# Latent attention: scores with keys on the partitions in three rounded passes, the row maximum as a 97th feature, sums and scalings on GpSimd

## The reference, cut to what matters

```python
def queries(cq, rotate):
    q = (_rms(cq) * q_norm) @ w_uq
    q = _rms(q.reshape(*q.shape[:2], MLA_HEADS, MLA_QK)) * q_gain
    return _rope_tail(q, cos, sin) if rotate else q

def _block_attention(q, k, v):            # scale = 96 ** -0.5
    s = jnp.einsum('bqhd,bkhd->bhqk', qi, k).astype(jnp.float32) * scale
    p = jax.nn.softmax(s, axis=-1).astype(v.dtype)
    return jnp.einsum('bhqk,bkhd->bqhd', p, v)
```

## Time and profile before

| what | us |
|---|---|
| median of 3 runs | 3493.1 (3488.01 to 3498.14) |
| the profiled execution | 3493.74 |
| its span, first to last instruction | 3492.4 |
| PE busy | 3274.6 (94%) |
| DVE / ACT / POOL busy | 1735.5 / 1314.0 / 1055.9 |
| queries' projection, PE at work without a gap, ends at | 2815.4 |
| first scores | 2823.85 |
| `mla_out_tensor` begins | 3068.37 |

### The profile page before, as it was taken

How to read it: one execution, slowest core, us unless ns; L and a number is a source line. 1 busy time by engine, 2 the same in 40 slices (tenths; PEclk the granted TensorE clock), 3 DMA queues, 4 the chain that set the end, 5 groups by cost and what they waited for, 6 DMA issues and landing times.

```text
span 3492.4 us, 44447 instructions
## 1 busy us (share of the span) xinstructions
PE 3274.6 (94%) x16968; PEld 2608.6 (75%) x16968; DVE 1735.5 (50%) x3222; ACT 1314.0 (38%) x2282; POOL 1055.9 (30%) x513
## 2 busy tenths in 40 slices
PE   8999999999999898999898899999999988889999
PEld 6677777777867777778786577888988556668877
DVE  5458445424138644532798655222565645543234
ACT  4433433333343334334424433222443455533332
POOL 3123131144313222124327332322543000034443
PEclk9999999999999899999999999999999999999999
DMA  5532121133462022123121001221332110022222
GB/s 184 194 127 80 52 89 46 61 101 117 156 227 86 33 71 83 55 83 124 64 67 61 1 31 61 67 67 61 121 109 85 38 36 1 8 72 91 97 97 79
DMA packets 87479, 286.40 MB, mean 82 GB/s; under 512 B 9697, under 2 KB 20321, under 8 KB 86497
## 3 DMA queue, kind: packets, MB, share of 16 engines
q1 hardware_dynamic: 85968, 272.67, 23.1%
q10 hardware_dynamic: 1296, 10.88, 0.8%
HBM read 279.31 MB, written 4.19 MB: 81 GB/s over the span
## 4 chain that ended last, share of the span: by engine, by line
PE 54%; DVE 7%; ACT 3%; issue 2%; POOL 0%; DMA 0%; DVEq 0%; ACTq 0%; POOLq 0%
PE psum L318 14%; PE psum L320 14%; PE psum L319 14%; PE psum L317 9%; PE psum L3796 1%; DVE mla_cols L3885 1%; PE psum L3784 1%; PE psum L1192 1%; DVE h_low L582 0%; PE psum L3762 0%; DVE padded L2834 0%; DVE ml_weights L3237 0%; DVE squares L511 0%; ACT weights_high L395 0%; ACT mla_probs L3841 0%
## 5 line engine op out<-in xcount | busy, mean ns | idle before, releaser
L413 POOL TENSOR_TENSOR weights_low<-weights_loaded,weights_high 128x1024 fp32r<-128x1024 f32 (+3 forms) x456 | 958.4, 2102 | 2350.3 <-ACT weights_high L395 2093.5
L318 PE MATMUL psum<-h_high,weights_high 128*128 128x512 f32 (+1 forms) x2384 | 901.0, 378 | 46.6 <-DVE h_low L582 21.2
L319 PE MATMUL psum<-h_low,weights_high 128*128 128x512 f32 (+1 forms) x2384 | 883.0, 370 | 0.0
L320 PE MATMUL psum<-h_high,weights_low 128*128 128x512 f32 (+1 forms) x2384 | 882.4, 370 | 0.0
L395 ACT CAST weights_high<-weights_loaded 128x1024 fp32r<-128x1024 f32 (+3 forms) x456 | 421.1, 923 | 463.0 <-PE psum L320 392.2
L318 PEld LDWEIGHTS psum<-h_high,weights_high 128*128 128x128 f32 x2384 | 456.2, 191 | 135.4 <-issue 32.6
L319 PEld LDWEIGHTS psum<-h_low,weights_high 128*128 128x128 f32 x2384 | 456.1, 191 | 77.8 <-issue 4.1
L320 PEld LDWEIGHTS psum<-h_high,weights_low 128*128 128x128 f32 x2384 | 454.8, 191 | 76.9
L318 PE MATMUL psum<-act_high,weights_high 128*128 128x512 f32 (+1 forms) x528 | 187.6, 355 | 8.2 <-DVE act_low L4183 6.2
L319 PE MATMUL psum<-act_low,weights_high 128*128 128x512 f32 (+1 forms) x528 | 187.5, 355 | 0.0
L320 PE MATMUL psum<-act_high,weights_low 128*128 128x512 f32 (+1 forms) x528 | 187.4, 355 | 0.0
(11 more groups left out here) (512 smaller groups left out, 5240.8 us busy)
## 6 DMA issues: line engine op xcount, KB each, us to landing
weights_loaded<-stream_dram SPq DMA_DIRECT2D x468, 512.0 KB, 3.3
weights_loaded<-stream_dram SPq DMA_DIRECT2D x80, 128.0 KB, 2.3
weights_loaded<-stream_dram SPq DMA_DIRECT2D x24, 384.0 KB, 3.0
weights_loaded<-stream_dram SPq DMA_DIRECT2D x8, 272.0 KB, 4.6
x<-x_dram SPq DMA_DIRECT2D x4, 512.0 KB, 7.4
arena_mem<-mem_dram ACTq DMA_DIRECT2D x2, 1024.0 KB, 5.9
x<-x_dram ACTq DMA_DIRECT2D x1, 2048.0 KB, 8.4
x_kept_dram<-x ACTq DMA_DIRECT2D x1, 2048.0 KB, 9.8
```

Source lines behind the costliest of these rows:

```text
L318: pe.matmul(out, a.high, b.high, start=start, stop=False)
L319: pe.matmul(out, a.high, b.low, start=False, stop=False)
L320: return pe.matmul(out, a.low, b.high, start=False, stop=stop)
L413: pool.tensor_tensor(self.low[s][:, 0:size], raw[:, 0:size], self.high[s][:, 0:size], ALU.subtract).then_inc(*g.event("weights_low").up(po ...
```

## The change

What it does:

1. **Scores** have keys on the partitions: a tile is one head and 128 keys against all 512 queries, 12 tiles a pair, 96 in all, in the order of `TILES` (two key tiles of head 0, two of head 1, and so on). Both operands are `Split` pairs, so a tile is three rounded passes of 512 columns. There is no transpose of the exponentials.
2. **Maximum**: PE makes scores with the high parts alone, queries on the partitions ("limit": 128x768, a pass of 512 and one of 256 columns, 8 a pair, all through banks 3 and 4); DVE takes the maximum of the row; four 1-column transposes make a row of the four maxima; ACT writes its negative as the 97th feature of the query (`"row"`), against ones in the key's 97th (`edges_scalar`).
3. **Features**: ACT writes the high part, DVE the low one. The 20 transposes of a pair alternate between banks 5 and 7 with the rows and the totals.
4. **Scale of queries**: it is put on the queries by POOL (`scaled_queries`, 8 instructions), group by group, and the query roots are made by groups. POOL also scales the keys (`keys_gpsimd`, 48 instructions).
5. **Sums**: POOL adds the exponentials' tiles (10 additions of 128x512 a pair); PE adds over the partitions with ones (`totals`); ACT makes exp(-ln(total)), DVE corrects it and multiplies (`finish`).
6. **Weighing**: bursts of four fp32 multiplications of 512 columns, three a pair.
7. **First pair**: features, limits and row of pair 0 stand inside the last two groups of the queries' projection (`first_steps`); these two groups use three banks.
8. **Last pair**: the low parts of `mla_w_out` stand behind all additions on POOL; the split of pair 6's output comes first, then 0 to 5.

```diff
@@ up_tensor
+        turn = few if c >= GROUPS - 2 else turn        # Turn(0, 3)
@@
+            for step in first_steps(c, n):
+                step_tensor(g, 0, *step)
@@
-UNITS = [(2 * pair + i, q) for pair in range(PAIRS) for q in range(QT) for i in range(2)]
+TILES = [(i, 2 * k + b) for k in range(TT // 2) for i in range(2) for b in range(2)]
+PER_PAIR, BURST = len(TILES), 4
+N_PROBS = 5
+FEATURE_BANKS, LIMIT_BANK, OUT_BANK = (5, 7), 3, 6
+def head_steps(n):
+    features = {0: [(0, 0), (0, 1)], 1: [(0, 2)], 2: [(1, 0)], 3: [(1, 1)], 4: [(1, 2)]}
+    return ([("features", i, step) for i, step in features.get(n, [])]
+            + ([("limit", (n - 4) // QT, n % QT)] if n >= 4 else []) + ([("row", 0, 0)] if n == 9 else []))
@@ heads_tensor
+        b = g.claim(key, key[1] % 3)
+        mm(g, g.banks(b), t.k_feat[h % 4][:, kt * P:(kt + 1) * P], t.q_feat[h % 4][:, :], True, True)
@@
+        for n in range(PER_PAIR if pair < PAIRS else BURST):
+            if pair < PAIRS:
+                scores(pair, n)
+            if n % BURST == 0 and pair + n:
+                at = (pair * PER_PAIR + n) // BURST - 1
+                weigh(at // (TT // 2), at % (TT // 2))
+            if pair < PAIRS and n == 0:
+                step_tensor(g, pair, "row", 1, 0)
+            if pair and n == BURST - 1:
+                totals(pair - 1)
+            if pair + 1 < PAIRS:
+                for what, i, x in head_steps(n):
+                    step_tensor(g, pair + 1, what, i, x)
@@ heads_scalar
+                exponentials(pair * PER_PAIR + n)
+                if n == 0:
+                    step_scalar(g, pair, "row", 1, 0)
+            if pair and n == BURST:
+                inverse(pair - 1)
@@
+            elif pair + 1 == PAIRS and 4 <= n < 4 + PAIRS - 1:
+                weighted_high_scalar(g, (n - 5) % (PAIRS - 1))
+                if n == 8:
+                    g.weights.round(("mla_w_out", 0))
@@ heads_vector, finish(pair), called at n == BURST before the steps
+        dve.tensor_tensor(total, total, r, ALU.mult).then_inc(*S("total").up(dve))
+        dve.scalar_tensor_tensor(r, total, -2.0, r, ALU.add, ALU.mult).then_inc(*S("drained").up(dve, key))
+        dve.scalar_tensor_tensor(out, out, -1.0, r, ALU.mult, ALU.mult).then_inc(*S("drained").up(dve, ("mla_out", pair)))
@@ heads_gpsimd, between ffn_gpsimd(0) and ffn_gpsimd(1)
+    g.weights.low_parts("mla_up")
+    for c in range(GROUPS):
+        keys_gpsimd(g, c)
+    for pair in range(PAIRS):
+        scaled_queries(g, pool, pair)
+    for n in range(PAIRS * PER_PAIR):
+        add(n)
```

More of the change, by code:

```diff
@@ L3624, in up_scalar @@
     act, S, t = g.act, g.event, g.t
+    g.weights.note("mla_up")
     nq, nk = mla_norms(g)
@@ new lines, in edges_scalar @@
+def edges_scalar(g, h):
+    act, S, t, one = g.act, g.event, g.t, g.ones[0:1, 0:1]
+    for part, n, scale in ((t.k_feat[h].high, TOK, 1.0), (t.k_feat[h].low, TOK, 0.0), (t.q_feat[h].low, SEQ, 0.0)):
+        ones = bass.AP(tensor=one.tensor, offset=one.offset, ap=[[one.ap[0][0], 1], [0, n]])
+        for m in g.after(act, *([S("head_sums").at(GROUPS * (TT + QT) - 1)] if h > 1 else [])):
+            act.wait_ge(*m)
+        act.activation(part[MLA_QK:MLA_QK + 1, :], ones, ACT.Copy, scale=scale).then_inc(*S("edged").up(act, h))
@@ new lines, in step_scalar @@
+def step_scalar(g, pair, what, i, x):
+    act, S, t, h = g.act, g.event, g.t, 2 * pair + i
+    if what == "features":
+        which, tiles = TURNS[x]
+        key, at = ("features", h, x), slice(tiles[0] * P, (tiles[-1] + 1) * P)
+        dst, gain = (t.k_feat, g.small.k_gain_col) if which == "k" else (t.q_feat, g.small.q_gain_col)
+        freed = [S("scored").at(("mla_tile", (pair - 1) * PER_PAIR - 1))] if pair >= 2 else []
+        freed += [S("head_sums").at(GROUPS * (TT + QT) - 1)] if pair == 1 else []
+        for m in g.after(act, S("projected").at(key), *freed):
+            act.wait_ge(*m)
+        act.activation(dst[h % 4].high[0:MLA_QK, at], g.bank(key)[0:MLA_QK, 0:len(tiles) * P], ACT.Copy,
+                       scale=gain).then_inc(*S("feature_high").up(act, (h, x)))
+    elif what == "row":
+        key = ("limit_row", h)
+        for m in g.after(act, S("projected").at(key)):
+            act.wait_ge(*m)
+        act.activation(t.q_feat[h % 4].high[MLA_QK:MLA_QK + 1, :], g.bank(key)[0:1, 0:SEQ], ACT.Copy,
+                       scale=-1.0).then_inc(*S("drained").up(act, key))
@@ new lines, in step_vector @@
+def step_vector(g, pair, what, i, x):
+    dve, S, t, h = g.dve, g.event, g.t, 2 * pair + i
+    if what == "features":
+        which, tiles = TURNS[x]
+        key, at = ("features", h, x), slice(tiles[0] * P, (tiles[-1] + 1) * P)
+        dst, gain = (t.k_feat, g.small.k_gain_col) if which == "k" else (t.q_feat, g.small.q_gain_col)
+        part = dst[h % 4][0:MLA_QK, at]
+        for m in g.after(dve, S("feature_high").at((h, x))):
+            dve.wait_ge(*m)
+        dve.scalar_tensor_tensor(part.low, g.bank(key)[0:MLA_QK, 0:len(tiles) * P], gain, part.high, ALU.mult,
+                                 ALU.subtract).then_inc(*S("drained").up(dve, key))
+    elif what == "limit":
+        key = ("limit", h, x)
+        freed = [S("projected").at(("limit_row", h - 2))] if h >= 2 else []
+        for m in g.after(dve, S("projected").at(key), *freed):
+            dve.wait_ge(*m)
+        dve.tensor_reduce(t.limits[h % 2][:, x:x + 1], g.bank(key, 2)[:, 0:TOK], AX_X, ALU.max).then_inc(
+            *S("drained").up(dve, key))
```

360 lines of the change are left out of this document (188 added, 172 removed).

## The result

The changed kernel takes 3509.3 us (median of 10 runs, 3498.7 to 3513.9) against 3492.6 for the kernel before (10 runs beside it): a ratio of 1.0048 with a 95% interval of 1.0033 to 1.0062. It is slower by 0.5%, 16.7 us, where I had forecast 3486 us, no measurable change. The profiled execution has a span of 3508.7 us at a mean granted clock of 0.961; before, 3492.4 at 0.971.

A forecast was written before the change was run, and what follows sets the result against it. A chain of waits through PE, DVE and ACT in the heads was taken as the bound; 10.2 + 8.1 + 28.0 + 6 x 28.1 + 30.5 = 245.4 against 253.0 us, so 3486 us, range 3456 to 3506.

The forecast's parts named there:

- the likeliest case: Worked schedule of waits through the heads: 28.1 us a pair, 3486 us in all, range 3476 to 3497, chance 0.48.
- rival 2: In each pair, between burst and tile 6, two PE waits lower the clock: 4 us a pair, up to 3514, chance 0.16.
- first pair, in the projection: Pair 0's steps inside the last two query groups: 4.4 us of PE work plus 5.8 of waits, 10.2 together.
- tail to the first scores: From the last query to the first scores, behind DVE's last operations and maxima: 8.1 us, close to 8.4 before.
- pair 0, tile 0 to tile 0: First pair in the heads: 26.0 us without totals or finish, plus 2.0 for the lower clock at its start.
- a pair at 2.4 GHz: A pair in the heads from the worked waits: 28.1 us, 1.25 less than now, ends 26 and 30.
- last pair: From the last pair to the output projection, bounded by ACT's exponentials: 30.5 us, bounds 27 and 34, 8.5 less than now.
- The pair's schedule: Waits inside a pair: PE idles 2.1 before the turning, 1.9 at the second limit, then rounds of 1.63; 28.1 us.
- Rival 1: Waits in the pairs mostly hidden by overlapping turnings and maxima: 23 to 25 us a pair, 3458 us, chance 0.24.
- Rival 3: GpSimd's additions late, first and last pair and DVE wait: 8 to 15 us more, 3494 to 3501, chance 0.08.
- Rival 4: Change fails to do what it says, e.g. two heads' weighings not side by side: 5.2 more a pair, 3505, chance 0.04.
- The signs that I had named: Same tile one pair later: 28 us means schedule, under 25 rival 1, over 31 with clock under 1.00 rival 2.

The follow-up runs named there:

- second filling: Changed kernel plus only 7 useless passes a pair in tile 5, where PE waits for the first maximum: 3490.9 us, ratio 0.9996, pair 29.12.
- the finish is split: Kernel with turning and finish later and limits from tile 3, plus finish operations singly behind three maxima and tile 6's limit before its turning: 3468.5 us, ratio 0.9937.
- the doubled additions: Changed kernel with each of GpSimd's 80 additions followed by a multiplication of the sum by one: 3514.3 us, ratio 1.0074, pair 32.05.
- first pair spread: Kernel with finish split, early first low part and early splits, plus first pair's limits spread further forward in the projection: 3477.0 us, ratio 0.9955.
- the three kernels with the same waits: Kernel with the finish split; that plus GpSimd's first output-weight low part early; that plus splits early: ratios 0.9937, 0.9919, 0.9936.
- ACT's splits earlier: Kernel with finish split and early first low part, plus last pair's output splits and ACT's output-weight rounding moved to earlier tiles: 3470.0 us, ratio 0.9936.

## Why the prediction was wrong, point by point

The step that failed is the choice of the likeliest case: that PE keeps 2.4 GHz through two waits of some 2 us, so that the clock's term in pairs 1 to 6 is 0. The runs showed 2.9 us a pair in its place, 18 of the 23 us by which the stretch was missed. That the clock falls there was on the page as rival 2, with the right place and mechanism and a chance of 0.16. Its row showed the lower clock behind a wait of 1.58, and I set it aside because the steady heads of before kept 1.00, though those have no such wait. The same trace has a longer wait 5.4 us earlier, which the prediction doesn't name:

```profile
3048.00 1.42 PE L3796 MATMUL psum<-mla_turned,mla_v 128*64 128x128 f32 x21 [2.12 <-ACT mla_turned L3856]
```

Behind it the granted clock was 1.00 (window 3048.0 to 3053.5), and it fell only behind the wait of 1.58. The rest of the terms:

| term | worked | measured |
|---|---|---|
| first pair, in the projection | 10.2 | 96.0 - 85.6 = 10.4 |
| tail to the first scores | 8.1 | 2833.80 - 2825.4 = 8.4 |
| pair 0, tile 0 to tile 0 | 28.0 | 2861.75 - 2833.80 = 27.95 |
| a pair at 2.4 GHz | 28.1 | 29.12 |
| clock, a pair | 0 (rival: 4) | 2.9 |
| pairs 1 to 6, together | 168.6 | 3054.67 - 2861.75 = 192.9 |
| last pair | 30.5 | 3083.38 - 3054.67 = 28.7, and 0.75 later |

(2825.4 is the last pass of the projection, started at 2824.9 and 0.49 long; 2861.75, 3054.67 are starts of tile 0.)

- **Two terms came out by luck.** Pair 0 was worked as 26.0 and 2.0 for the lower clock at its start. The kernel with the second filling has the same start and no fall in the pair, and takes 25.8 in all; the 2.2 more of the changed kernel are a fall behind the wait of 1.63 at 2847.31, which the sum did not have. In the first pair's 10.2 the waits were 5.0 (worked 5.8), so the rest is 5.4 (worked 4.4).
- **The pair's schedule** was right in its parts: the turning at t + 13.55 (worked 13.4), the second limit at t + 16.9 (16.7). It was 1.0 short mainly because a round takes 1.74 and not 1.63 (2890.51 to 2892.25): beside DVE's 0.96 the hand-overs are 0.78, where I had worked 0.67. Six rounds are 0.7 of it; the other 0.3 is open. 6 x 1.0 = 6 us of the miss of 23.
- **The clock's price** was mis-sized in the rival: 2.9, not 4. From the second limit to the first behind the burst it is 9.8 in the pair shown (2878.63 to 2888.43) and 6.6 at 2.4 GHz (2904.92 to 2911.48 with the second filling): 1.7 for the burst and 0.4 for each of some three rounds. I had let the clock stay down for the rounds behind the burst too, and it didn't. 6 x 2.9 = 18 us; less the 1.8 of the last pair the two come to 22 of the 23. The rival's own sum was loose: at 4 us a pair two pairs, not six, outweigh the gain of 7.6.
- **Rival 1** (waits hidden, 23 to 25 a pair) does not happen in the kernel as changed, but the price was near: 25.6 once the finish is split. By seven pairs its times are 3450 to 3464, not 3451 to 3467.
- **Rival 3** (GpSimd late) is refuted by the doubled additions, inside the pairs. **Rival 4** is refuted by the trace: the two heads' weighings start 0.01 apart (2862.55 and 2862.56 in the changed kernel) and eight take 1.94.
- **DVE beside GpSimd**: the maxima took 0.958 us at most, all 64, though GpSimd adds beside many of them, while the low parts with two inputs in SBUF went from 0.69 to 1.61. Both agree with the rule of the Trainium skill quoted in the prediction ("SBUF — State Buffer", "Who interferes with whom"). The Trainium skill, "TensorE: Matmul & The Clock Gate", section "A second HAM failure mode: psum-queue depth-cycling", has short idle times between groups of matmuls in cycling banks bring the clock down. Here one fall is of that kind, that of "first pair spread" behind waits of 0.42; the 18 pairs of the three kernels with the same waits stayed at 1.00, and the falls in the pairs of the changed kernel come at or behind waits of 1.6 to 1.7.
- **Last pair**: PE waits 1.45 and 2.72 for exponentials in it, the wait at the first low part is there (1.35) and that at the last head pair (0.75); 1.8 shorter than worked. That ACT bounds it, as the prediction has it, fits these waits, but no run shows it: with ACT's splits earlier it was 1.0 longer.

The signs that I had named came out on the side of rival 2: over 31 a pair with a clock under 1.00. PE waiting for L3981 and L3960 was a sign of the schedule and of rival 2 alike, and held.

## What to carry to other kernels

When a change halves an engine's work inside a loop with hand-overs, price every wait that then appears twice: as idle time, and as what the clock does behind it. Here PE's waits of 1.2 to 2.2 us inside the pairs 1 to 6 came with a fall in every pair, but for the one kernel that kept only the wait for the finish. A block of operations on the engine that others wait for is moved in pieces that fit its own gaps, one between two, or the wait only moves. Useless passes in a wait are a cheap test of the clock: if more work makes it faster and the granted clock goes up with it, it is the clock. Look at where in the trace the clock falls before naming what makes it fall.

## What was not expected of the hardware

- Two waits of nearly the same length, 1.69 and 1.63, stand 3 us apart in a pair. With the first alone the granted clock stays at 1.00 in six pairs, with the second alone it falls in six. With both it falls up to 1 us behind the second in four pairs and already at its start in two. Neither the length of the wait nor the short waits behind it decide it by themselves; what does, these runs don't settle.
- One wait in one place can do either. The wait of 1.76 for the first pair's feature (2801.95 in the changed kernel) stands in the same code in eleven of the changed kernels. In five of their executions the next query tile runs at the lower clock for 3 us (its eight passes take 4.15 in the kernel with the finish split), in six it doesn't (2.75).
- The low clock ends by itself in the middle of the same work, after 7 to 10 us in the changed kernel, and comes back in each pair; its length differs between otherwise equal pairs (31.1 to 32.7 us a pair).
- A GpSimd operation of 128x512 with two full inputs takes 1.27, the same size with one input repeated from a column 1.04.
- An addition of GpSimd takes 1.60 instead of 1.27 while DVE's two-input low parts run, and those 1.57 instead of 0.69: both are slowed.
